# Gated linear attention: levels' products issued two levels at a time, the outputs' products regrouped, and one empty step moved in an earlier normalisation

## The chip, the core and the metric

The kernel runs on one core of a Trainium2 chip. The metric is the device time of one execution in microseconds, the median of several runs. TensorE (PE) does the matrix products and writes them to PSUM, which has 8 banks; VectorE (DVE) and ScalarE (ACT) read PSUM, do the elementwise work and prepare the operands; SyncE (SP) starts the weight transfers.

## The reference, cut to what matters

Three transformer blocks follow one another on 1024 tokens of width 1024. All three end in an MLP. The second block has a causal convolution branch whose output goes through a layer norm, a SiLU and an RMS norm; the third has gated linear attention (4 heads, keys of 64, values of 128). The parts that the change touches:

```python
# second block, convolution branch: h is normalised twice
y = silu(layer_norm_2(conv(u * sigmoid(gate)) + conv_b, ln_g, ln_b))
mix = concatenate([rms_norm_2(a, attn_out_g), rms_norm_2(y, conv_out_g)])

# third block, gated linear attention, per head
S_t = diag(exp(gk_t)) @ S_{t-1} + k_t^T v_t
o_t = q_t @ S_t
# in chunks: o = (masked, decayed q k^T) @ v  +  (q * exp(b)) @ S
#            S = S * exp(b_last) + (k * exp(b_last - b))^T v
```

## The kernel before, in words

**The walk.** The tokens are worked in two halves of 512. Each engine walks through one common list of steps, written out by hand. A step may hold a "unit" (one slab of weights: 24 matmuls over 512 tokens and what evicts them) and the keys of "segments", which are generators that do one slice of a mixer or norm on each engine. On every engine the segments' slice of a step comes first, then the splitting of the weights of the unit two ahead (ACT writes w_hi at L258, DVE writes w_lo at L263), then the unit. While one half goes through its MLP (units "up", L314 on PE, evicted by ACT at L344 to L349 and DVE at L359; units "down", L292, evicted by DVE at L364), the other half's next block is worked beside it: `merge` gives each step without a unit of its own one of these MLP units. An AIR step is one with no segment, so that it holds only an MLP unit. DVE waits in every step for the unit's products, and so enters the next step only after PE has finished the unit.

**Gated linear attention** (segment "gla", two halves of four chunks of 128 tokens, n = 0 to 7). The decayed product of queries and keys is built in eight levels: in level l, blocks of 128 >> (l+1) tokens attend to the blocks before them, and level 7 is the diagonal. A chunk takes GLA_PERIOD = 10 steps, t = 0 to 9. At step t DVE makes the level's exponents (`away`, level t), the operands ql and kl of level t-1 (`operands`, L2696 and L2698) and copies under a mask the product of level t-2 into A (`pick`, L2707). PE does level t-2 (`level`, L2595): four heads, each a product over 64 of the 128 partitions (heads 0 and 2 on the lower 64, heads 1 and 3 on the upper), 128 columns wide, in f32, which makes two instructions of it. Even levels go to PSUM banks 4 and 5, odd ones to 6 and 7; the lower rows write the first and the upper rows the second of the two. At t = 3 two transposes of the decayed keys (L2627) into bank 4 go ahead of level 1; ACT copies them out (L2656). At t = 0 of the next chunk PE does the `output`: head by head a product of A and the values over all 128 partitions (L2605), and at once the one of the state over 64 partitions (L2606); then two products over 128 partitions for the new state (L2610). All eight levels and the output stand ahead of the step's MLP unit.

**The convolution branch's norms** (segment "cnorm", nine slices, once in each half, in the second block beside the first and second MLPs). PE adds over the channels with a product of 512 f32 columns (L2176) in slices 1, 3 and 6. The third sum needs what ACT squares (L2216) and DVE folds (L2233, L2238) in slice 5, after ACT's SiLU (L2212) in slice 4. After the third sum come Ln and Exp on ACT (L2199, L2201), the scaling on DVE (L2262), and the split of the mixed activations (L386, L391) in slices 6 to 8; the output projection's units follow.

```python
steps += alone(((("cnorm", h),), 7)) + AIR + alone(((("cnorm", h),), CN_STEPS - 7))   # slices 0..6, empty, 7, 8
```

Of the kernel before, what the change touches and what calls it, by code (L numbers as in the profile page):

```python
# [32 lines left out]
GH = 4  # L33
# [87 lines left out]
def build_program(nc, g):  # L121

    ctx = ExitStack()
    with ctx:
# [2047 lines left out]
        CN_STEPS = 9  # L2172
# [98 lines left out]
        LP, LK, LV = 2, 64, P  # L2271
# [288 lines left out]


        GLA_PERIOD = LL + 3
        GLA_STEPS = GLA_PERIOD * HB + 1

        def each(n, per=1, j=0):
            return per * n + (j + 1)

        def quarter(b, h):
            return ps[:, b + h % 2, (h // 2) * P:(h // 2 + 1) * P]
# [7 lines left out]
        def gla_pe(pe, h):  # L2577
            w = l_w[h]

            def level(n, c, l):  # L2580
                pe.wait_ge(gl["lq"], gl0["lq"] + each(n, LL + 1, l))
                if l < LL:
                    pe.wait_ge(gl["lk"], gl0["lk"] + each(n, LL, l))
                if l >= 2:
                    pe.wait_ge(gl["pred"], gl0["pred"] + each(n, LL + 1, l - 2))
                if l == 2:
                    pe.wait_ge(gl["ketc"], gl0["ketc"] + each(n))
                if l == 0 and n:
                    pe.wait_ge(gl["osc"], gl0["osc"] + n)
                if l == 1 and n:  # L2590
                    pe.wait_ge(gl["end"], gl0["end"] + n)
                for i in range(GH):
                    rows = slice(LK * (i % 2), LK * (i % 2) + LK)
                    keys = w["kl"][l % 2][rows, i // 2, :] if l < LL else l_k[rows, i // 2, META + c * P:META + (c + 1) * P]
                    last = nc.tensor.matmul(quarter(4 + 2 * (l % 2), i), keys, w["ql"][l % 2][rows, i // 2, :], start=True, stop=True)  # L2595
                last.then_inc(gl["lA"], 1)

            def output(n, c):
                pe.wait_ge(gl["pred"], gl0["pred"] + each(n, LL + 1, LL))
                pe.wait_ge(gl["qd"], gl0["qd"] + each(n))  # L2600
                if n:
                    pe.wait_ge(gl["end"], gl0["end"] + n)
                for i in range(GH):
                    rows = slice(LK * (i % 2), LK * (i % 2) + LK)
                    nc.tensor.matmul(quarter(4, i), l_vt[:, c, i * LV:(i + 1) * LV], w["A"][n % 2][:, i, :], start=True, stop=False)  # L2605
                    last = nc.tensor.matmul(quarter(4, i), l_S[rows, i // 2, :], w["qd"][rows, i // 2, :], start=False, stop=True)  # L2606
                last.then_inc(gl["out"], 1)
                pe.wait_ge(gl["ketc"], gl0["ketc"] + each(n))
                for j in range(LP):
                    last = nc.tensor.matmul(ps[:, 6 + j, 0:256], w["ket"][:, j, :], l_vt[:, c, j * 256:(j + 1) * 256], start=True, stop=True)  # L2610
                last.then_inc(gl["su"], 1)

            for c in range(HB):
                n = HB * h + c
                if c:
                    output(n - 1, c - 1)
                else:
                    for e in g3s[h][GH - 2:]:
                        own_free(pe, e)
                    if h == 0:  # L2620
                        pe.wait_ge(l_meta, 7)
                for t in range(GLA_PERIOD):
                    if t == 3:
                        pe.wait_ge(gl["ked"], gl0["ked"] + each(n))
                        pe.wait_ge(gl["pred"], gl0["pred"] + each(n, LL + 1, 0))
                        for j in range(LP):
                            last = nc.tensor.transpose(ps[:, 4, j * P:(j + 1) * P], w["ke"][:, j, :], const("ident"))  # L2627
                        last.then_inc(gl["tr"], 1)
                    if t >= 2:
                        level(n, c, t - 2)  # L2630
                    yield
            output(HB * h + HB - 1, HB - 1)
            yield

        def gla_act(act, h):
            w = l_w[h]

            for c in range(HB):
                n = HB * h + c
                tok = slice(META + c * P, META + (c + 1) * P)  # L2640
                for t in range(GLA_PERIOD):
                    if t == 0:
                        act.wait_ge(gl["kdiff"], gl0["kdiff"] + each(n))
                        nc.scalar.activation(w["ke"][:, :, :], w["ke"][:, :, :], ACT.Exp, scale=GATE).then_inc(gl["ke"], 1)
                        nc.scalar.activation(w["eb"][:, :, :], l_b[:, :, tok], ACT.Exp, scale=GATE).then_inc(gl["eb"], 1)
                    if t == 1:
                        if n:
                            act.wait_ge(gl["end"], gl0["end"] + n)
                        nc.scalar.activation(l_small[:, L_LAST, 0:LP].unsqueeze(2), l_b[:, :, tok.stop - 1:tok.stop], ACT.Exp, scale=GATE)\
                            .then_inc(gl["last"], 1)  # L2650
                    if t < LL:
                        act.wait_ge(gl["neg"], gl0["neg"] + each(n, LL, t))
                        nc.scalar.activation(w["e"][t % 2][:, :, :], w["e"][t % 2][:, :, :], ACT.Exp, scale=GATE).then_inc(gl["exp"], 1)  # L2653
                    if t == 3:
                        act.wait_ge(gl["tr"], gl0["tr"] + each(n))
                        nc.scalar.activation(w["ket"][:, :, :].rearrange("p j x -> p (j x)"), ps[:, 4, 0:LP * P], ACT.Copy).then_inc(gl["ketc"], 1)  # L2656
                    yield
            yield

        def gla_dve(dve, h):  # L2660
# [41 lines left out]
            def pick(n, l):  # L2702
                dve.wait_ge(gl["lA"], gl0["lA"] + each(n, LL + 1, l))
                if l:
                    dve.wait_ge(gl["pred"], gl0["pred"] + each(n, LL + 1, l - 1))
                nc.vector.memset(l_small[:, L_WAIT, 0:1], 0.0)
                nc.vector.copy_predicated(by_bank(w["A"][n % 2][:, :, :]), l_mask[:, l, :].unsqueeze(1).unsqueeze(1).to_broadcast([P, 2, LP, P]),  # L2707
                                          two_banks(4 + 2 * (l % 2))).then_inc(gl["pred"], 1)

            for c in range(HB):  # L2710
                n = HB * h + c
                tok = slice(META + c * P, META + (c + 1) * P)
                q, k, b = l_q[:, :, c * P:(c + 1) * P], l_k[:, :, tok], l_b[:, :, tok]
                for t in range(GLA_PERIOD):
                    if t == 0:
                        if c:
                            finish(n - 1, c - 1)
                        else:
                            for e in g3s[h][GH - 2:]:
                                unit_done(dve, e)  # L2720
                            dve.wait_ge(l_scan, 2 * h + 2)
                            for i in range(2):
                                nc.vector.memset(w["A"][i][:, :, :], 0.0)
                        nc.vector.tensor_tensor(w["ke"][:, :, :], b[:, :, P - 1:P].to_broadcast([P, LP, P]), b, ALU.subtract)\
                            .then_inc(gl["kdiff"], 1)
                    if t == 1:
                        dve.wait_ge(gl["ke"], gl0["ke"] + each(n))
                        nc.vector.tensor_tensor(w["ke"][:, :, :], w["ke"][:, :, :], k, ALU.mult).then_inc(gl["ked"], 1)
                        dve.wait_ge(gl["eb"], gl0["eb"] + each(n))
                        nc.vector.scalar_tensor_tensor(w["qd"][:, :, :], q, scale, w["eb"][:, :, :], op0=ALU.mult, op1=ALU.mult)\  # L2730
                            .then_inc(gl["qd"], 1)
                    if t < LL:
                        away(n, b, t)
                    if 1 <= t <= LL + 1:
                        operands(n, q, k, t - 1)
                    if t >= 2:
                        pick(n, t - 2)
                    yield
            finish(HB * h + HB - 1, HB - 1)
            yield  # L2740
# [225 lines left out]
        def alone(*keys_steps):  # L2966
            return [(None, keys) for keys, n in keys_steps for _ in range(n)]
# [29 lines left out]
        def block2(h):  # L2997
# [13 lines left out]
                    done += 1  # L3011
            steps += AIR + block
            steps += alone(((("conv2", h),), CK - done))
            steps += alone(((("cnorm", h),), 7)) + AIR + alone(((("cnorm", h),), CN_STEPS - 7))
            steps += [(u, ()) for u in out2[h]]
            steps += alone(((("rms_mlp2", h),), RMS_STEPS))
            return steps
# [283 lines left out]
```

## Time and profile before

| what | value |
|---|---|
| median of 3 runs | 3879.99 us (3878.58 to 3883.11) |
| the profiled execution | 3878.06 us |
| its span in the profile | 3876.3 us |
| PE busy | 3825.1 us, 99% of the span |
| DVE, ACT busy | 2204.4 us (57%), 1568.4 us (40%) |
| mean granted clock of TensorE | 0.997 of full speed |

All durations below come from this one execution. The profiled execution is 1.8 us longer than its span, and 1.9 us under the median. In the chain of work a piece's length is the time until the next piece begins, so that the pieces add up to the span; in the timeline and the groups a matmul's duration runs to the end of its pass through the array and overlaps with the next.

### The profile page before, as it was taken

To read this page: it belongs to the slowest core of one execution; us is meant where nothing else is said; L and a number is where in the kernel's file an instruction comes from. 1 tells how busy PE (TensorE), PEld (TensorE's weight loads), DVE (VectorE), ACT (ScalarE), POOL (GpSimd) and SP (SyncE) were. 2 spreads that over 40 slices of the span, in tenths; PEclk is the share of its full clock that TensorE was granted. 3 is DMA by queue.
4 is the path that set the end of the run, shared out by engine and by line. 5 is a ranking of instruction groups with operands and counts; after the bars stand their busy time and mean duration, and the time that the engine had idled before them with its cause. 6 is when DMAs were issued, how large, how long until landed. Compare 5 with 4: busy or idle time off the path is not lost.

```text
span 3876.3 us, 49150 instructions
## 1 busy us (share of the span) xinstructions
PE 3825.1 (99%) x20434; PEld 3080.0 (79%) x20434; DVE 2204.4 (57%) x3353; ACT 1568.4 (40%) x2510; POOL 17.1 (0%) x34
## 2 busy tenths in 40 slices
PE   8999999999999999999999999999999999999998
PEld 5777788778888878878888789877787877788887
DVE  5631787766534658747578655266556256545334
ACT  5441555544333534445444433333334233334333
POOL 0000000000000000000000000000000000000000
PEclk9999999999999999999999999999999999999999
DMA  5122000042422222222222222222222222223222
GB/s 191 44 71 59 10 7 15 26 133 93 120 94 97 93 87 77 87 87 93 93 77 82 94 92 90 91 82 77 76 97 90 90 83 81 79 90 117 96 92 87
DMA packets 113971, 323.55 MB, mean 83 GB/s; under 512 B 27016, under 2 KB 34136, under 8 KB 113752
## 3 DMA queue, kind: packets, MB, share of 16 engines
q1 hardware_dynamic: 111512, 314.91, 24.5%
q0 software_dynamic: 2240, 5.51, 0.7%
q8 instruction: 163, 2.67, 0.3%
q14 instruction: 56, 0.46, 0.0%
HBM read 303.86 MB, written 18.06 MB: 83 GB/s over the span
## 4 chain that ended last, share of the span: by engine, by line
PE 95%; DVE 2%; ACT 2%; issue 1%; DMA 0%; SPq 0%; DVEq 0%; ACTq 0%
PE ps L314 52%; PE ps L292 27%; PE ps L1155 2%; PE ps L1467 2%; PE ps L1161 1%; PE ps L1444 1%; PE ps L728 1%; PE ps L2595 1%; PE ps L928 1%; PE ps L2030 1%; PE ps L1452 1%; DVE g_D L1343 0%; ACT n_s L1499 0%; PE ps L1250 0%; DVE n_s L1557 0%
## 5 line engine op out<-in xcount | busy, mean ns | idle before, releaser
L314 PE MATMUL ps<-a,w_hi 128*128 128x512 f32 (+1 forms) x6064 | 1846.6, 389 | 2.5 <-ACT l_vf L2437 0.8
L314 PEld LDWEIGHTS ps<-a,w_hi 128*128 128x128 f32 x6064 | 1110.6, 188 | 266.2 <-issue 16.4
L314 PE MATMUL ps<-a,w_lo 128*128 128x512 f32 (+1 forms) x3032 | 1148.3, 385 | 0.0
L263 DVE TENSOR_TENSOR w_lo<-w_raw,w_hi 128x1024 fp32r<-128x1024 f32 x539 | 658.2, 1221 | 407.7 <-ACT w_hi L258 405.1
L258 ACT ACTIVATE w_hi<-w_raw 128x1024 fp32r<-128x1024 f32 x539 | 563.6, 1050 | 518.5 <-DMA w_raw<-in_w_mlp 321.4
L314 PEld LDWEIGHTS ps<-a,w_lo 128*128 128x128 f32 x3032 | 563.1, 188 | 120.3
L292 PE MATMUL ps<-h_hi,w_hi 128*128 128x512 f32 x1536 | 490.4, 401 | 0.0
L292 PE MATMUL ps<-h_hi,w_lo 128*128 128x512 f32 x1536 | 480.8, 395 | 0.0
L292 PE MATMUL ps<-h_lo,w_hi 128*128 128x512 f32 x1536 | 480.5, 394 | 0.0
L359 DVE TENSOR_TENSOR h_lo<-u_sq,h_hi 128x512 fp32r<-128x512 f32 x192 | 132.9, 692 | 483.8 <-ACT h_hi L349 483.8
L364 DVE TENSOR_TENSOR xT<-xT,ps 128x1024 f32<-128x1024 f32 x192 | 234.2, 1220 | 269.3 <-PE ps L292 268.4
L292 PEld LDWEIGHTS ps<-h_hi,w_hi 128*128 128x128 f32 x1536 | 285.2, 188 | 72.0 <-issue 7.2
L292 PEld LDWEIGHTS ps<-h_hi,w_lo 128*128 128x128 f32 x1536 | 289.3, 188 | 65.6
L292 PEld LDWEIGHTS ps<-h_lo,w_hi 128*128 128x128 f32 x1536 | 289.3, 188 | 65.1
L344 ACT ACTIVATE u_act<-ps 128x512 f32<-128x512 f32 x128 | 76.5, 598 | 363.9 <-PE ps L314 363.8
L2003 DVE SCALAR_TENSOR_TENSOR mixh<-c_pad,params,mixh 128x512 f32<-128x512 f32 x240 | 163.7, 745 | 0.0
L348 ACT ACTIVATE u_sq<-u_act 128x512 f32<-128x512 f32 x192 | 121.4, 632 | 18.1 <-ACT u_act L344 0.8
L344 ACT ACTIVATE u_act<-ps,params 128x512 f32<-128x512 f32 x64 | 44.0, 688 | 203.5 <-PE ps L314 203.5
L349 ACT ACTIVATE h_hi<-u_act 128x512 fp32r<-128x512 f32 x192 | 118.0, 615 | 0.0
L370 DVE TENSOR_TENSOR xT<-xT,ps 128x512 f32<-128x512 f32 x48 | 32.9, 686 | 137.2 <-PE ps L314 137.2
L2653 ACT ACTIVATE l_e<-l_e 128x256 f32<-128x256 f32 x56 | 23.4, 418 | 144.8 <-DVE l_e L2689 143.7
L438 ACT ACTIVATE a<-mixh 128x512 fp32r<-128x512 f32 x64 | 40.5, 633 | 80.0 <-DVE mixh L453 78.8
(367 smaller groups left out, 3190.3 us busy)
## 6 DMA issues: line engine op xcount, KB each, us to landing
w_raw<-in_w_mlp SPq DMA_DIRECT2D x384, 512.0 KB, 3.3
w_raw<-in_w_in SPq DMA_DIRECT2D x107, 512.0 KB, 3.3
w_raw<-in_w_out SPq DMA_DIRECT2D x48, 512.0 KB, 3.3
xT<-in_x SPq DMA_DIRECT2D x8, 512.0 KB, 8.2
x<-xT SPq DMA_DIRECT2D x2, 2048.0 KB, 8.1
xT<-x SPq DMA_DIRECT2D x2, 2048.0 KB, 11.0
rpb_rows<-in_rpb SPq DMA_DIRECT2D x1, 3810.0 KB
z<-staged SPq DMA_DIRECT2D x4, 512.0 KB, 3.7
```

What stands on the lines that cost most here:

```text
L258: nc.scalar.activation(w_hi[u.z][:, :], w_raw[u.z][:, :], ACT.Copy).then_inc(w_hi_done[u.z], 1)
L263: nc.vector.tensor_tensor(w_lo[u.z][:, :], w_raw[u.z][:, :], w_hi[u.z][:, :].bitcast(F32), ALU.subtract).then_inc(w_split[u.z], 1)
L292: last = nc.tensor.matmul(ps[:, u.bank + c, :], w[:, k * 256 + c * P:k * 256 + (c + 1) * P], act[:, (u.first + k) % RING, :], start=(k == ...
L314: last = nc.tensor.matmul(ps[:, bank, 0:t1 - t0], w[:, k * P:(k + 1) * P], a[:, h, low, k, t0:t1], start=(i_k == 0 and i == 0), stop=(i_k ...
L344: nc.scalar.activation(u_act[:, s, :], ps[:, u.bank, :], ACT.Relu, bias=bias).then_inc(bank_free(u), 1)
L348: nc.scalar.activation(u_sq[:, s, :], u_act[:, s, :], ACT.Square)
L349: nc.scalar.activation(h_hi[:, u.chunk % RING, :], u_act[:, s, :], ACT.Square).then_inc(hid_hi, 1)
L359: nc.vector.tensor_tensor(h_lo[:, r, :], u_sq[:, u.chunk % 2, :], h_hi[:, r, :].bitcast(F32), ALU.subtract)\
L364: nc.vector.tensor_tensor(two, two, ps[:, u.bank:u.bank + 2, :], ALU.add).then_inc(bank_free(u), 1)
L1155: last = nc.tensor.matmul(pbank(b)[:, h, :], lhsT[:, h, :], rhs[:, h, :], start=start, stop=stop)
L1467: last = nc.tensor.matmul(ps[:, 7, c * P:(c + 1) * P], n_pt[c][:, t, :], v, start=(t == 0), stop=(t == KR // 2 - 1))
L2003: nc.vector.scalar_tensor_tensor(y, x, w, y, op0=ALU.mult, op1=ALU.add).then_inc(c_tap, 1)
```

## The change

The levels' products are done by twos: at t = 3, 5, 7 and 9 PE does levels t-3 and t-2 one after the other, and none at the other steps. The transposes and ACT's copy of them go from t = 3 to t = 2. `pick` of a level follows one step later than before (level t-3 at step t), and the last step picks levels 6 and 7. The waits go with them: level 0 waits for ACT's copy of the transposes, which shares bank 4, and the transposes wait for DVE's copy of the output. In `output` the four heads' products of A and the values stand together, then the four of the state. In the second block the AIR step goes from behind the cnorm slice of the third sum to ahead of it.

```diff
+        LEVELS_AT = range(3, GLA_PERIOD, 2)
...
-                if l == 2:
+                if l == 0:
                     pe.wait_ge(gl["ketc"], gl0["ketc"] + each(n))
-                if l == 0 and n:
-                    pe.wait_ge(gl["osc"], gl0["osc"] + n)
...
+                for i in range(GH):
+                    nc.tensor.matmul(quarter(4, i), l_vt[:, c, i * LV:(i + 1) * LV], w["A"][n % 2][:, i, :], start=(i < 2), stop=False)
                 for i in range(GH):
                     rows = slice(LK * (i % 2), LK * (i % 2) + LK)
-                    nc.tensor.matmul(quarter(4, i), l_vt[:, c, i * LV:(i + 1) * LV], w["A"][n % 2][:, i, :], start=True, stop=False)
-                    last = nc.tensor.matmul(quarter(4, i), l_S[rows, i // 2, :], w["qd"][rows, i // 2, :], start=False, stop=True)
+                    last = nc.tensor.matmul(quarter(4, i), l_S[rows, i // 2, :], w["qd"][rows, i // 2, :], start=False, stop=(i >= 2))
...
-                    if t == 3:
+                    if t == 2:
                         pe.wait_ge(gl["ked"], gl0["ked"] + each(n))
-                        pe.wait_ge(gl["pred"], gl0["pred"] + each(n, LL + 1, 0))
+                        if n:
+                            pe.wait_ge(gl["osc"], gl0["osc"] + n)
...
-                    if t >= 2:
+                    if t in LEVELS_AT:
+                        level(n, c, t - 3)
                         level(n, c, t - 2)
...
-                    if t == 3:
+                    if t == 2:
                         act.wait_ge(gl["tr"], gl0["tr"] + each(n))
...
-                    if t >= 2:
-                        pick(n, t - 2)
+                    if t >= 3:
+                        pick(n, t - 3)
+                    if t == LL + 2:
+                        pick(n, LL)
...
-            steps += alone(((("cnorm", h),), 7)) + AIR + alone(((("cnorm", h),), CN_STEPS - 7))
+            steps += alone(((("cnorm", h),), 6)) + AIR + alone(((("cnorm", h),), CN_STEPS - 6))
```

## Rows read from the trace of the kernel before

**Rows 1.** The page: busy time, share of the span, instructions.

```profile
PE 3825.1 (99%) x20434; PEld 3080.0 (79%) x20434; DVE 2204.4 (57%) x3353; ACT 1568.4 (40%) x2510; POOL 17.1 (0%) x34
```

**Rows 2.** Chain of work in the linear attention: start, length, piece.

```profile
2547.07 0.65 PE ps L2595 x8
2547.72 5.70 PE ps L292 x24
...
2585.52 0.22 PE ps L2605 x2
2585.74 0.41 PE ps L2606 x2
2586.16 0.42 PE ps L2605 x2
...
2588.66 1.06 PE ps L2610 x4
2589.72 11.00 PE ps L292 x48
...
2607.07 0.22 PE ps L2627 x2
```

**Rows 3.** Chain of work in the second block's attention.

```profile
1999.08 1.93 PE ps L2057 x16
2001.01 5.72 PE ps L292 x24
2006.73 0.44 PE ps L2038 x4
2007.16 5.51 PE ps L292 x24
```

**Rows 4.** Groups by line, PE: count, busy us, mean ns, idle before.

```profile
L2595 PE MATMUL ps<-l_ql,l_kl 64*128 64x128 f32 x448 | 40.1, 297 | 0.0
L2595 PE MATMUL ps<-l_ql,l_k 64*128 64x128 f32 x64 | 5.7, 297 | 0.0
L2606 PE MATMUL ps<-l_qd,l_S 64*128 64x128 f32 x64 | 15.5, 322 | 0.0
```

**Rows 5.** Timeline of PE, one level: start, length, idle before.

```profile
2547.00 0.71 PE L2595 MATMUL ps<-l_ql,l_kl 64*128 64x128 f32 x8
```

**Rows 6.** Waits of PE over the whole span: us, times, longest.

```profile
PE ps L2176 <- DVE c_sq L2238: 6.2, 2, 3.3
```

**Rows 7.** Timeline around both third sums and behind the first.

```profile
1665.61 0.39 PE L314 MATMUL ps<-a,w_lo 128*128 128x512 f32 x1
1669.31 1.13 PE L2176 MATMUL ps<-c_sq,consts 128*128 128x512 f32 x2 [3.31 <-DVE c_sq L2238]
1677.42 0.63 PE L292 MATMUL ps<-h_hi,w_hi 128*128 128x512 f32 x2
1689.96 2.49 DVE L391 TENSOR_TENSOR a<-mixh,a 128x512 fp32r<-128x512 f32 x4
1694.22 0.62 PE L314 MATMUL ps<-a,w_hi 128*128 128x512 f32 x2
2190.91 0.39 PE L314 MATMUL ps<-a,w_lo 128*128 128x512 f32 x1
2194.14 1.12 PE L2176 MATMUL ps<-c_sq,consts 128*128 128x512 f32 x2 [2.84 <-DVE c_sq L2238]
2200.66 0.63 PE L292 MATMUL ps<-h_hi,w_hi 128*128 128x512 f32 x2
```

**Rows 8.** Chain of work around the first half's second sum.

```profile
1648.46 0.86 PE ps L2176 x2
1649.32 5.58 PE ps L314 x24
```

**Rows 9.** Stretch behind the first third sum; PEclk is the granted clock.

```profile
1669.30:1674.40 5.10, 5.09 (x14) 3.70 (x15) 4.24 (x6) 4.05 (x7) 0.00 (x0) 0.67 0.00 0
```

**Rows 10.** One step beside an up unit, DVE and ACT.

```profile
2740.45 0.60 ACT L344 ACTIVATE u_act<-ps 128x512 f32<-128x512 f32 x1 [1.61 <-PE ps L314]
2744.14 0.42 DVE L2698 TENSOR_TENSOR l_kl<-l_e,l_k 128x256 f32<-128x256 f32 x1
2744.24 0.37 ACT L2656 ACTIVATE l_ket<-ps 128x256 f32<-128x256 f32 x1
2744.48 0.75 DVE L2707 COPY_PREDICATED l_A<-l_mask,ps 128x512 f32<-128x512 int32 x1
```

## Prediction

> **What bounds the kernel now.** I began with the page's busy times: PE is busy for 3825.1 us of a span of 3876.3, DVE and ACT for 57% and 40% [rows 1]. So I read the rest as an account of PE's time. A microsecond taken off PE counts in full as long as the other engines keep up, and a microsecond taken off DVE counts nothing. "Busy" does not say that the array is well used, so next I followed the chain of work through the linear attention. It never leaves PE there: level, MLP unit, level, MLP unit [rows 2]. PE's list of waits has nothing from this segment; the groups of level products show 0.0 us of idle time [rows 4]. A gain here can only come from PE doing the same products in less time. The one wait that the change touches is in the list: the third sum of cnorm, 6.2 us in two waits [rows 6].
>
> **What a visit to 64-row products costs.** A down unit takes 11.00 / 2 = 5.50 us when no level stands before it, and 5.70 us behind a level, which itself takes 0.65 us [rows 2]. One level costs 0.65 + 0.20 = 0.85 us. How much of it is work? The second block's attention has the same kind of product, 64 rows, alternating in the same way, but 16 instructions of twice the columns: 1.93 + (5.72 - 5.51) = 2.14 us [rows 3]. Let x be the time of one 128-column instruction and F what a visit costs whatever it holds. Then 8x + F = 0.85 and 32x + F = 2.14, so x = 0.054 us and F = 0.42 us. Half of what a level costs is entering and leaving. Products over all 128 rows pay nothing of the kind: four transposes between two units take 0.44 us, and the unit behind them 5.51 us [rows 3], so 0.11 us each.
>
> The output confirms it without my two equations. There 128-row and 64-row pairs alternate, with no wait between them: the first pair takes 0.22, each later one 0.41 or 0.42, though one pair is 0.22 of work [rows 2]. That is 0.20 for each change of kind, in or out, 0.40 for a visit.
>
> **Part 1, the levels by twos.** There are 512 level instructions [rows 4], 8 to a level, so 64 visits. By twos there are 32: the work is the same, 32 visits go, 32 x 0.42 = **13.4 us**. Bounds: nothing below, if each level paid for itself whatever stands beside it; the rows of the output speak against this. A milder doubt: eight starts within 0.71 us, the last of them 0.27 us long, are 0.063 us apart [rows 5], which fits x with the pairing of the rows but also a floor on how fast instructions start. With a floor of 0.063, F is 0.85 - 0.50 = 0.35 and the part gives 32 x 0.35 = 11.2 us. I take 13.4.
>
> **Part 2, the transposes alone at t = 2.** They cost 0.22 us ahead of a level now [rows 2] and, being 128-row products, 0.22 us alone: nothing gained, nothing lost.
>
> **Part 3, the outputs.** Now: 0.22 + 0.41 + 6 x 0.416 + 1.06 = 4.19 us from the first pair to the unit, in each of eight chunks [rows 2]. Afterwards: eight A instructions at 0.108 are 0.87; the eight state instructions now alternate lower and upper rows as the levels do, 8 x 0.054 = 0.43; one visit is 0.42; the two products for the state (four instructions), without the change of kind that their 1.06 now contains, are 0.86. The sum is 2.58. The gain is 1.61 us a chunk, **12.9 us** in all. If the state's products did not overlap, 0.43 less each: 9.5 us, the lower bound; nothing in the rows would make it more than 12.9. The flags of start and stop move, which costs no instruction.
>
> The Trainium skill, TensorEngine Tiling, section Tiling Modes, says that changing the tiling mode, not only the tile, drains TensorE; that is the same cause as my F. Its page TensorE: Matmul & The Clock Gate gives a fixed part of about 166 ns to a lone matmul at full clock (section Single matmul latency). An estimate from that page, two drains a visit, is 0.33 us instead of the 0.42 of the rows; with 56 visits fewer (32 in part 1, 24 in part 3), parts 1 and 3 would then give some 22 us instead of 26. The rows have the duration, so they decide.
>
> **Part 4, the empty step.** The third sum waits for DVE. In the first half the last product before it starts at 1665.61; one more of 0.23 and the sum could start at 1665.84, but it starts at 1669.31: 3.47 us. From there to the next unit it takes 1677.42 - 1669.31 = 8.11 us, where the second sum and its unit take 0.86 + 5.58 = 6.44 [rows 7, 8]. The other 1.67 us are the granted clock, 0.67 on average in the 5.1 us behind the wait [rows 9], between the levels of 1.2 and 2.4 GHz, after PE had been idle. In the second half: 2194.14 - 2191.14 = 3.00 us, then 2200.66 - 2194.14 = 6.52 us, 0.08 too much. Together 5.14 + 3.08 = **8.2 us**. With one more unit of 5.6 us ahead of it the sum starts 2.1 us after its data in the first half, 2.6 in the second, so the whole 8.2 goes. What is late next? Slices 7 and 8 now follow slice 6 directly. Slice 6 comes 2.2 us later against its data, and DVE's chain behind it (Ln, Exp, four scalings, two batches of splits) still runs slice by slice, held by PE's units: the second batch ends at 1692.45 for an output projection that begins at 1694.22 and wants its last chunk 4.9 us after that [rows 7]. That cover, 1.8 us at the first chunk and 6.7 at the last, stays, because slices 7 and 8 keep their distance to the projection.
>
> **Do DVE and ACT keep up?** Each level goes to PE with operands made a step earlier. Beside an up unit, the tightest kind, the step that PE's unit ended at 2740.4 has kl ready at 2744.56 (4.2 us later), ACT's copy of the transposes at 2744.61 and the pick at 2745.23 (4.8 us) [rows 10]. PE now takes 6.44 us to the next level, and after the change 5.6 in a step without products: 1.4 us of cover remain for kl and for the copy, which level 0 now waits for, and 1.2 for the pick that the second of two levels waits for, because the first one's 0.4 us go ahead. ACT is idle for 1.61 us ahead of the next eviction [rows 10], and loses 0.85. Two picks in the last step add 0.75 to an end some 2.9 us ahead of its use. I cost all this at nothing. If the cover were missing by a microsecond in the 24 pairs whose second level has a new-found pick to wait for (levels 3, 5, 7 in eight chunks), it would cost 24 us.
>
> **Sum.** 13.4 + 0 + 12.9 + 8.2 = 34.5 us against the profiled execution: 3878.06 - 34.5 = 3843.6. That execution is 1.9 us under the median, so the median should be **3845.5 us**, 0.9% faster. What this kernel's measurement can tell from no change is about 0.2%, 7.8 us.
>
> **Rivals.**
> - *The price is per level, not per visit*: what I call F would be paid by the semaphore or the bank change of each level. Against it: the output pays it with no wait between the pairs. Then 3845.5 + 13.4 = 3858.9. Chance 7%.
> - *No overlap among the state's products, or a floor on starts*: 3.4 and 2.2 us less, 3848 to 3851. The level rows, the same shapes in the same banks, speak against the first. Chance 6%.
> - *The empty step only moves the wait*: the projection or slice 6 waits instead for what the third sum waited for. It gives 3853.7. The covers of 1.8 and 6.7 us speak against. Chance 4%.
> - *No change*: PE's visits shrink but its gain is taken by DVE, on which it then waits; needs waits of 34 us in all where there are none today. 3880. Chance 2%.
> - *Slower*: the second level of a pair waits for its pick. The pick's cover shrinks from over 6 us (it was made two steps ahead) to 1.2 us. It decides from the point at which the pick is (34.5 + 7.8) / 24 = 1.8 us beyond its cover, 3.0 us later than in the rows; it would give 3888 and more. Chance 1%.
> - *As forecast*: 80%.
>
> **Range.** Down, the terms are near their ceilings; the run-to-run spread of before (3878.6 to 3883.1) and F taken from rounded rows (0.02 over 56 visits, 1 us) give 3840. Up, it takes in the two milder rivals and reaches to the first one: 3859. So 3840 to 3859. Faster 97%, same 2%, slower 1%.
>
> **What the new profile would show.** The level groups would stand as 16 instructions, in the chain about 16 x 0.054 + 0.2 = 1.07 us, with a unit of 5.70 or 5.79 us behind; steps without levels would show units of 5.50 and 5.58. The output: eight A instructions in 0.87, eight of the state in 0.6 to 0.7, then 1.06; on the timeline the state's group as one of eight. The wait of L2176 gone from PE's list, the granted clock 1.00 there. What would make me wrong: levels' groups of 16 at 1.5 us; an idle time before L2595 released by DVE L2707 or ACT L2656; a wait for L391 before the projection of the second block.

## The result, and the profile after

The changed kernel takes 3844.58 us (median of 4 runs, 3843.8 to 3846.63), the kernel before 3880.63 in the same set. The ratio is 0.991, 95% interval 0.9895 to 0.9924: faster by 0.9%, some 36 us. The forecast was 3845.5 in 3840 to 3859. The profiled execution took 3843.8 us, its span is 3842.0: 34.3 us shorter than that of before. (The two medians differ by 36.1 us; the four runs of before spread over 4.5 us.)

The chain of work in the linear attention, changed kernel (start, length, piece), answers to [rows 2]:

```profile
2539.93 3.67 PE ps L292 x16
2543.60 1.09 PE ps L2595 x16
2544.69 5.70 PE ps L292 x24
2550.39 5.56 PE ps L314 x24
2555.95 1.09 PE ps L2595 x16
2557.04 11.36 PE ps L314 x48
2568.39 1.09 PE ps L2595 x16
2569.49 5.79 PE ps L314 x24
2575.28 0.89 PE ps L2605 x8
2576.17 0.65 PE ps L2608 x8
2576.82 1.06 PE ps L2612 x4
```

Read it in pairs. A group of one level took 0.65 us, a group of two takes 1.09, not 1.30: the second level adds 0.44 us, 0.055 for each of its eight instructions. The unit behind a group still has its 0.20 us on top (5.70), but half as often. In the output, A's eight instructions take 0.89 and the state's eight 0.65, exactly one level group; the whole is 2.60 us against 4.19.

For the sum over a half I use one stretch that no wait at the start of the kernel disturbs: from the sums that follow the linear attention of the first half (L2749 before, L2755 after) to those of the second. It holds one of the two attention halves. For the other half I count from the products of the first state (L2525). From the chain of the kernel before:

```profile
2516.20 1.05 PE ps L2525 x4
...
2800.65 3.43 PE ps L2749 x8
...
3389.84 3.43 PE ps L2749 x8
```

and of the changed kernel:

```profile
2507.63 1.05 PE ps L2525 x4
...
2779.38 3.43 PE ps L2755 x8
...
3355.59 3.43 PE ps L2755 x8
```

The stretch takes 589.19 us before and 576.21 after, 12.98 less; the first half takes 284.45 and 271.75, 12.70 less. Together 25.7 us. In the experiments below, "for both halves" means twice the difference of the stretch, which for this reason can be off by some 0.3 us.

The chain around the third sum of the first half, changed kernel, answers to [rows 7, 8]:

```profile
1648.73 0.86 PE ps L2176 x2
1649.59 22.24 PE ps L314 x96
1671.84 0.86 PE ps L2176 x2
1672.69 16.49 PE ps L292 x72
1689.19 10.89 PE ps L314 x47
```

There is no gap between the second sum and the third, with four up units (x96) between them instead of three. The second half reads the same, with its second sum at 2168.57 and the end of the three down units at 2209.02:

```profile
2168.57 0.86 PE ps L2176 x2
...
2192.53 16.49 PE ps L292 x72
```

The window around the first of the two third sums:

```profile
1665.00:1677.00 12.00, 12.00 (x52) 9.46 (x51) 8.37 (x11) 11.18 (x17) 0.00 (x0) 1.00 0.25 87
```

PE is busy all 12.00 us and the granted clock (third number from the end) is 1.00, where [rows 9] had 0.67. The two waits of [rows 6] are gone from PE's list, and nothing of L2595, L2605 or L2608 has come into it.

### The profile page after: what moved, and what is told of

The parts are those of the page before. It is cut to its first block, busy times and chain, and to the rows that moved or that the text cites. A ratio compares the mean times of both kernels' runs of the same rounds, so it can differ in the third digit from the quotient of the medians.

```text
span 3842.0 us, 49141 instructions
## 1 busy us (share of the span) xinstructions
PE 3796.8 (99%) x20434; PEld 3071.5 (80%) x20434; DVE 2202.8 (57%) x3353; ACT 1567.7 (41%) x2510; POOL 17.1 (0%) x34
## 4 chain that ended last, share of the span: by engine, by line
PE 96%; DVE 2%; ACT 1%; issue 1%; DMA 0%; SPq 0%; DVEq 0%; ACTq 0%
PE ps L314 53%; PE ps L292 27%; PE ps L1155 2%; PE ps L1467 2%; PE ps L1161 1%; PE ps L1444 1%; PE ps L728 1%; PE ps L2595 1%; PE ps L928 1%; PE ps L2030 1%; PE ps L1452 1%; DVE g_D L1343 0%; ACT n_s L1499 0%; PE ps L1250 0%; DVE n_s L1557 0%
```

## The experiments

Each was timed in 4 to 11 runs beside the kernel before, whose medians there were 3879.4 to 3880.2. "Plus" is against the changed kernel's 3844.6, and "stretch" is the one above, against its 576.21 us.

**The empty step back behind the third sum** (changed kernel otherwise).

```diff
-            steps += alone(((("cnorm", h),), 6)) + AIR + alone(((("cnorm", h),), CN_STEPS - 6))
+            steps += alone(((("cnorm", h),), 7)) + AIR + alone(((("cnorm", h),), CN_STEPS - 7))
```

> The changed kernel with the empty step put back behind the third sum's slice. If the wait and the lower clock behind it are the whole of this part, the time is the changed kernel's 3844.6 plus 8.2 us = 3852.8, with waits of about 3.3 and 2.8 us on L2176 and a granted clock under 1 behind the first of them. Rival: only the waits count (6.2 us), the clock would have dropped anyway: 3850.8. Rival: the time lost in the wait is made up elsewhere: 3844.6.

Measured: 3855.0, plus 10.4; stretch 576.27, unchanged as it must be. The first wait in its timeline and the clock behind it:

```profile
1665.96 0.39 PE L314 MATMUL ps<-a,w_lo 128*128 128x512 f32 x1
1669.65 2.07 PE L2176 MATMUL ps<-c_sq,consts 128*128 128x512 f32 x2 [3.30 <-DVE c_sq L2238]
...
1678.85 0.63 PE L292 MATMUL ps<-h_hi,w_hi 128*128 128x512 f32 x2
```

```profile
1669.30:1674.40 5.10, 4.75 (x9) 3.13 (x10) 3.29 (x5) 3.68 (x7) 0.00 (x0) 0.50 0.00 0
```

The wait is as long as before (3.46 us from 1666.19), but this time the clock is at its lower level for the whole stretch behind it (0.50 of full speed, 1.2 GHz): 1678.85 - 1669.65 = 9.20 us where 6.44 are due, 2.76 us lost instead of 1.67. So the price beyond the wait's length differed between these two executions, at the same length; the rival that counts only the waits is out. From the second sum to the end of the third down unit this run takes 46.99 us in the first half and 43.90 in the second, where the changed kernel takes 40.45: 10.0 us more. That is the 8.2 expected, 1.1 for the longer stretch at the lower clock, and 0.6 in the three down units of each half, which take 16.80 us here and 16.49 in the changed kernel (see part 4 below).

**The outputs head by head again.**

```diff
                 for i in range(GH):
-                    nc.tensor.matmul(quarter(4, i), l_vt[:, c, i * LV:(i + 1) * LV], w["A"][n % 2][:, i, :], start=(i < 2), stop=False)
-                for i in range(GH):
                     rows = slice(LK * (i % 2), LK * (i % 2) + LK)
-                    last = nc.tensor.matmul(quarter(4, i), l_S[rows, i // 2, :], w["qd"][rows, i // 2, :], start=False, stop=(i >= 2))
+                    nc.tensor.matmul(quarter(4, i), l_vt[:, c, i * LV:(i + 1) * LV], w["A"][n % 2][:, i, :], start=True, stop=False)
+                    last = nc.tensor.matmul(quarter(4, i), l_S[rows, i // 2, :], w["qd"][rows, i // 2, :], start=False, stop=True)
```

> The changed kernel with the outputs' products head by head again, A and state in turn. Visit theory (0.20 us for each change between 128-row and 64-row products, and the state's products of two heads overlap once they stand together): plus 12.7 us, 3857.3. Rival, overlap is nothing and only the changes of kind count: 24 visits of 0.42 = 10.1, 3854.7. Rival, the order does not matter: 3844.6.

Measured: 3858.3, plus 13.7; stretch 582.60, plus 6.39, that is 12.8 for both halves and 1.60 us a chunk. The rival without overlap (10.1) misses by more than the spread.

**The levels one at a time**, with the outputs regrouped and the empty step moved: the kernel before with only the two other edits.

> The kernel before with the outputs regrouped and the empty step moved, but the levels one at a time and the transposes ahead of level 1. Visit theory: 32 visits more than the changed kernel, from its own rows (1.09 + 0.20 against 2 x 0.85) 0.41 us each, plus 13.1 us, 3857.7. Rival with a floor of 0.063 us on starts: plus 11.2, 3855.8. Rival, the price is per level: 3844.6.

Measured: 3857.8, plus 13.2; stretch 582.78, plus 6.57. The first half, read from L2525 as above, takes 278.03 instead of 271.75, plus 6.28. Together 12.9 us: 0.40 us for each of 32 visits. The price per level is ruled out as the only cause, and the floor of 0.063 us (11.2) does not fit the stretch.

**Heads in the order 0, 2, 1, 3.**

```diff
-                for i in range(GH):
+                for i in (0, 2, 1, 3):
                     rows = slice(LK * (i % 2), LK * (i % 2) + LK)
```

> The changed kernel with the heads of a level in the order 0, 2, 1, 3, so that two heads on the same 64 rows follow each other. Nothing else changes, the number of visits stays. If 0.054 us an instruction comes from products on the lower rows running beside those on the upper ones, then four instructions on the same rows take 0.32 us of their own where two took 0.11: 16 instructions take 1.28 instead of 0.86, plus 0.3 to 0.4 us a pair of levels, 32 pairs, plus 10 to 13 us, 3855 to 3858. If 0.054 to 0.063 is a floor on how fast instructions start, whatever rows they use: 3844.6, no change.

Measured: 3848.7, plus 4.1; stretch 577.90, plus 1.69, 3.4 for both halves. Neither expectation holds. A group takes 1.19 us instead of 1.09:

```profile
2555.87 1.19 PE ps L2595 x16
```

Either products on the upper and lower rows overlap over more than their neighbours, or they do not need to overlap at all. That called for the next run.

**All heads on the lower rows.** Heads 1 and 3 take the keys and queries of heads 0 and 2, so that part of the computation is replaced.

```diff
                 for i in range(GH):
-                    rows = slice(LK * (i % 2), LK * (i % 2) + LK)
+                    rows = slice(0, LK)
```

> The changed kernel with all four heads of a level taken from the lower 64 rows, so that heads 1 and 3 work on the keys and queries of heads 0 and 2: a part of the computation is replaced, the number and the shapes of the instructions stay. The order 0, 2, 1, 3 cost only 0.10 us a pair where my model of the overlap wanted 0.3 to 0.4. Theory 1: products on the lower rows do run beside those on the upper ones, and PE holds enough instructions ready that the order of the heads hardly matters. Then without any upper rows 16 instructions take 16 x 0.107 = 1.7 us of their own instead of 0.9, plus 0.8 us a pair, 32 pairs, plus 26 us, about 3871. Theory 2: a product over 64 rows simply takes half as long as one over 128, 0.054 us, wherever it lies: 3844.6, no change.

Measured: 3873.3, plus 28.7; stretch from 2791.47 to 3381.88, 590.41, plus 14.20. The group:

```profile
2555.65 1.98 PE ps L2595 x16
```

1.98 us, 0.89 more: the 16 x 0.107 = 1.71 of work that theory 1 wanted, and 0.27 on top. So a 64-row product is as slow as a 128-row one; what halves it is the one on the other rows beside it. The Trainium skill, TensorEngine Tiling (Array Packing), section Key Properties, says that different tiles can work in parallel; the trace agrees, 1.09 against 1.98 us. My picture of it, in which only direct neighbours overlap, was wrong.

The timeline shows the overlap directly, in a window that closes some 0.1 us after the first product of a group. The changed kernel, 2555.85:2556.00:

```profile
2555.88 0.38 PE L2595 MATMUL ps<-l_ql,l_kl 64*128 64x128 f32 x2
```

The order 0, 2, 1, 3, window 2555.70:2555.90:

```profile
2555.80 0.39 PE L2595 MATMUL ps<-l_ql,l_kl 64*128 64x128 f32 x2
```

All heads on the lower rows, window 2555.50:2555.70:

```profile
2555.58 0.37 PE L2595 MATMUL ps<-l_ql,l_kl 64*128 64x128 f32 x1
```

One product of this kind has 0.37 us, and two together have 0.38 or 0.39, so the two start within 0.02 us of each other; with all heads on the lower rows there is one, and the next starts at 2555.79. Starts 0.02 us apart also rule out a floor of 0.063 on starts. The weight loads start in pairs in the same way, and these runs do not tell apart what their overlap gives and what that of the products gives.

**A 128-row product between the two levels of a pair.**

```diff
+                if l % 2:
+                    nc.tensor.transpose(ps[:, 6, 256:384], const("ident"), const("ident"))
                 for i in range(GH):
```

> The changed kernel with one transpose of the identity (128 rows, two instructions) put between the two levels of each pair; its result is used by nothing, it only makes PE change from 64 rows to 128 and back. The transpose itself costs 0.22 us, 32 times 7.0 us. Visit theory: 32 visits come back at 0.41 us, 13.1 more, together plus 20 us, 3864.7. Rival, the price belongs to each level (semaphore, banks), not to the change of rows: plus 7.0, 3851.6.

Measured: 3858.3, plus 13.7; stretch 583.45, plus 7.24, 14.5 for both halves. The pair in its chain:

```profile
2556.43 0.65 PE ps L2597 x8
2557.08 0.26 PE ps L2593
2557.33 0.65 PE ps L2597 x8
```

My expectation had the transpose wrong: it is one instruction, 0.11 us, as the two of [rows 2] should have told me (0.22 for two transposes), not two for 0.22. With 32 x 0.11 = 3.5 the visit theory wants 3.5 + 13.1 = 16.6 and the rival 3.5. The measured 14.5 leaves 11.0 for 32 visits, 0.34 each. Both levels are back at the 0.65 of a level on its own, though their semaphores, banks and step are those of the pair. The change of rows is shown as the cause; a visit cut by a single 128-column product is a little cheaper than one between units of 512 columns (0.40). Why, these runs do not say.

**Levels by fours**: 0 to 3 at t = 5, 4 to 7 at t = 9.

```diff
-        LEVELS_AT = range(3, GLA_PERIOD, 2)
+        LEVELS_AT = range(5, GLA_PERIOD, 4)
...
-                if l >= 2:
-                    pe.wait_ge(gl["pred"], gl0["pred"] + each(n, LL + 1, l - 2))
+                if l >= 4:
+                    pe.wait_ge(gl["pred"], gl0["pred"] + each(n, LL + 1, (l - 4) | 2))
...
-                    last = nc.tensor.matmul(quarter(4 + 2 * (l % 2), i), keys, w["ql"][l % 2][rows, i // 2, :], start=True, stop=True)
+                    last = nc.tensor.matmul(quarter(4 + 2 * (l % 2), i, half_bank(l)), keys, w["ql"][l % 4][rows, i // 2, :], start=True, stop=True)
...
-                dve.wait_ge(gl["lA"], gl0["lA"] + each(n, LL + 1, l))
+                dve.wait_ge(gl["lA"], gl0["lA"] + each(n, LL + 1, l | 2))
```

> The changed kernel with the levels by fours: levels 0 to 3 at t = 5, 4 to 7 at t = 9, four buffers for ql and kl, two levels in the two halves of each PSUM bank. A pick waits for the second level of its banks, and four picks stand in the last step. Visit theory: 16 visits fewer, 0.41 us each, minus 6.5 us, 3838.1, with groups of 32 instructions of about 1.95 us in the chain. Rival, the output now waits for the last of four picks on DVE (cover about 1.9 us beside an up unit by the rows, so it should not), or level 4 for picks: 3844 or more. Rival, nothing is left to gain beyond two: 3844.6.

Measured: 3839.1, minus 5.5, ratio to the kernel before 0.9894 (0.9879 to 0.9909); stretch from 2778.03 to 3351.33, 573.30, minus 2.91, 5.8 for both halves, somewhat less than the 6.5 of the visit theory. It beats both kernels by medians: its runs (3837.7 to 3839.5) lie below all of the changed kernel's, though the two ratios' intervals overlap. The groups and the steps between them:

```profile
2544.13 1.99 PE ps L2601 x32
2546.11 5.70 PE ps L292 x24
2551.81 16.68 PE ps L314 x72
2568.49 1.99 PE ps L2601 x32
2570.47 5.79 PE ps L314 x24
```

1.99 us for four levels against 2 x 1.09, and one unit fewer that has 0.20 us on top. No wait for a pick came into PE's list.

**A late pick**: 2 us of memsets on DVE ahead of the pick at t = 4, 6, 8.

```diff
+                    if t in (4, 6, 8):
+                        for i in range(4):
+                            nc.vector.memset(w["idle"][:, i, :], 0.0)
                     if t >= 3:
                         pick(n, t - 3)
```

> The changed kernel with four memsets of 128x512 ahead of the pick at t = 4, 6 and 8 on DVE, about 1.7 us that does nothing for the result: it moves the pick for which the second level of a pair waits. By the rows the cover beside an up unit is 1.2 us, beside a down unit over 2.4 us. If that is right, PE waits about 0.5 us before some of the second levels beside up units, at most 24 of them, some 12 beside up units: plus 3 to 10 us, with idle time before L2595 released by DVE L2711. Rival, the cover is larger than 1.7 us: 3844.6 and no such wait. Rival, DVE falls behind from step to step: plus 20 us and more.

Measured: 3854.0, plus 9.4; stretch from 2784.87 to 3365.75, 580.88, plus 4.67. PE's waits have one new line:

```profile
PE ps L2597 <- DVE l_A L2713: 7.1, 8, 0.9
```

The memsets took 2.1 us, not 1.7. One of the eight places, PE and DVE of this run:

```profile
2620.31 0.71 PE L2597 MATMUL ps<-l_ql,l_kl 64*128 64x128 f32 x8
2621.93 0.71 PE L2597 MATMUL ps<-l_ql,l_kl 64*128 64x128 f32 x8 [0.90 <-DVE l_A L2713]
```

```profile
2619.03 2.11 DVE L2744 MEMSET l_idle<- 128x512 f32 x4
2621.06 0.72 DVE L2713 COPY_PREDICATED l_A<-l_mask,ps 128x512 f32<-128x512 int32 x1
```

The second level starts 1.62 us behind the first instead of some 0.55, 1.07 us late for a pick that came 2.1 us late: a cover of 1.0 us, where I had 1.2. Between the end of the pick (2621.78) and the start of the level (2621.93) lie 0.15 us, which I had not counted. The same place in the changed kernel:

```profile
2617.94 0.75 DVE L2711 COPY_PREDICATED l_A<-l_mask,ps 128x512 f32<-128x512 int32 x1
```

```profile
2619.36 1.16 PE L2595 MATMUL ps<-l_ql,l_kl 64*128 64x128 f32 x16
```

The pick ends at 2618.69 and the second level is due at about 2619.9, the 1.2 us of the forecast. So PE does wait when the pick is late, as the rival says that has the kernel slower, and the change stays one microsecond away from it, at eight places out of 24.

## Why the prediction was right, point by point

- *PE is the only account that counts.* It held: after the change PE's list of waits has no line of the levels' or the output's products, and the two attention halves gave 25.7 us, against 26.3 forecast for levels and outputs.
- *A visit costs 0.42 us, found from two group sizes.* Measured 0.40 (levels by one); the estimate of 0.33 us that stood beside it was too low. The further instruction at 0.054 measured 0.055 in the changed kernel and 0.056 by fours ((1.99 - 1.09) / 16). A pair of equations from two kinds of group told the visit within 0.02 us and the instruction within 0.002.
- *Part 1, 13.4 us*: 12.9 in the two halves, 13.2 by medians. The floor rival (11.2) fell.
- *Part 2, nothing*: the transposes stand alone at 0.22 us.
- *Part 3, 12.9 us*: 12.8 in the stretches, 13.7 by medians. The state's products do overlap, as the lower-rows run shows for the same shapes.
- *Part 4, 8.2 us, was a little small.* From the second sum to the end of the third down unit behind the third sum, the kernel before took 45.92 us in the first half and 43.87 in the second, the changed one 40.45 in both: 5.47 + 3.42 = 8.9 us. Of this, 8.3 are the waits and the clock; the other 0.6 are the three down units that follow, 16.80 us before and 16.49 after, a term that the sum did not have:

```profile
1669.31 1.13 PE ps L2176 x2
1670.44 7.15 PE ps L314 x24
1677.58 16.80 PE ps L292 x72
...
2173.76 0.86 PE ps L2176 x2
...
2200.83 16.80 PE ps L292 x72
```

  (the chain of the kernel before). The granted clock was 1.00 over these units in both kernels, so it is not the reason. What goes with it is the product that stands ahead: the chain of the kernel before has three down units in a row behind a transpose at 5.50 us each,

```profile
1586.21 0.44 PE ps L2038 x4
1586.65 16.50 PE ps L292 x72
```

  and those in a row behind an up unit at 5.60 each. The changed kernel has the sum ahead of them and no up unit. Why a whole row of down units keeps the pace of its beginning is open. The wait was worth still more in the run that put it back, because the clock stayed down longer.
- *Nothing else becomes late.* Held; the cover forecast at 1.2 us measured 1.0, because 0.15 us pass between the pick and the level.
- *The sum*: 34.5 us forecast, 25.7 + 8.9 = 34.6 in the two accounts, 34.3 between the spans. The other 0.3 us is in the front of the kernel: the changed kernel reaches the second sum of cnorm at 1648.73, 0.27 us later than the kernel before, and over all these profiles that moment lies between 1646.70 and 1650.60. The closeness is partly luck: the attention gave 0.6 us less than forecast and the empty step 0.7 more.

What was wrong did not reach the sum: the picture of how the products overlap, which predicted 10 to 13 us for another order of the heads where 3.4 to 4.1 came.

## What to carry to other kernels

When one engine never idles, look for changes of mode in its chain: solve the cost of a group for a fixed part and a part per instruction from two groups of different size, and put work of one mode (here: products over 64 or over 128 rows) together until the fixed part is small. Products over half the rows pay only when others on the other half stand near them, and the order among them matters little. Each such regrouping spends cover of the engine that reads the results, so work out the new distance before taking the next step (four levels at a time still had enough), and give an empty step to the place whose data are late, since a wait can also cost clock behind it.

## What the runs showed of the hardware that I had not expected

- Four products in a row on the same 64 rows cost almost nothing (1.19 against 1.09 us for 16), while 16 on the same rows cost nearly double (1.98 us). In the order 0, 2, 1, 3 the four instructions of heads 0 and 2, all on the lower rows, stand first in the program, and yet two products start within 0.02 us, where products on the same rows start at least 0.11 us apart. The records do not name the head, but by this PE looks further ahead than the neighbouring product for one on free rows.
- A wait of the same length (3.3 us) was followed by a mean granted clock of 0.67 in one execution and 0.50 in another over the same 5.1 us, and one of 2.8 us by no loss of clock (1.00 in the window below, kernel before, second half): 1.67, 2.76 and 0.1 us lost.

```profile
2194.00:2200.00 6.00, 5.86 (x24) 4.46 (x25) 5.13 (x8) 4.09 (x7) 0.00 (x0) 1.00 0.00 0
```

- Down units behind an up unit took 5.60 us each, as many as followed in a row, and 5.50 behind a sum or a transpose, at a granted clock of 1.00.
- A transpose of 128 f32 columns is one instruction of 0.11 us (two of them are L2627 x2, 0.22 us), where a plain f32 product of the same size is two (four heads are L2605 x8, 0.89 us).
